# Two transformer blocks on one core: how the relative position bias reaches the attention scores

## The chip, the cores and the metric

The kernel runs on one core of a Trainium2 chip. The metric is the device time of one execution in microseconds (us). The time before is a median of three runs. One further execution was profiled, and every row below is of that execution.

## What is computed

The input x has 256 tokens (T) of 1024 features (D). A first block applies attention and then a mixture of 32 experts (4 chosen per token). A second block applies a gated recurrent mixer, a convolution and a feed-forward part of 2816 features. All is float32. The change touches the attention of the first block alone. Cut to what matters, with 8 heads (H) of 128 features and 256 tokens, it is this:

```python
q, k, v = split(x @ w_in)                       # per head h: 256 x 128 each
s = (q @ k.T) * Dh ** -0.5 + rel_t[h, t5_bucket(qpos - kpos)]
s = where(qpos - kpos >= 0, s, -inf)
p = softmax(s, axis=-1)
t = (p @ v) @ w_out
```

The bias of a head depends on the distance between query and key only, so a head has one row of 512 numbers over all distances. What the products need is that row shifted by one place from query to query: a table of 256 keys for each of 128 queries of a tile.

## The kernel before, in words

The five engines each run a program written out by hand, and wait for each other on semaphores. Time runs through these stages.

**Projections and attention (0 to about 125 us).** The input projection is cut into 12 pieces of 256 columns, r = 0 to 11, in the order q, k, v for each of four pairs of heads (PAIRS). A piece comes by DMA from SP's queue into a ring in SBUF. It is split for exact products: ScalarE rounds it (`split_hi`, L1047), VectorE takes the rest (`split_lo`, L1334). TensorE forms three products per block of 128 (`product`, L562), in two halves of 48 products. Between the halves of the pieces TensorE does the attention of the pairs that are ready: `scores` of a pair in the middle of piece 3 and of the pieces 5, 8 and 11, `turn_probs` (transposes, L544) in the middle of piece 4 and of the later q pieces, `values` (L597, L598) after that. The last pair's transposes stand among the output products (`out_part`, L651).

`scores(h)` (L570) makes both query tiles of a head: queries 0 to 127 see 128 keys, queries 128 to 255 see 256 keys, so a head fills 384 columns of one PSUM bank. Each part has two products into the same bank: a matrix with ones on the anti-diagonal (`const("flip")`) by the bias table (L576, L578), and q by k on top of it (L577, L579). The flip is there because the bias table in SBUF lies with its queries in reverse order. VectorE then takes the row maximum from the bank (`row_max`, L1366, L1367), ScalarE reads the bank, subtracts the maximum, takes the exponential and writes `prob` in SBUF, summing on the way (`exps`, L1077, L1078), VectorE divides by the sum (`normalise`, L1373 to L1375), TensorE transposes.

**The bias table.** TensorE makes the 8 rows of 512 from the buckets (L611), VectorE adds the mask and leaves them in SBUF on 8 partitions (`rel_tab`, L1357). POOL's DMA queue stores them to a scratch tensor in device memory (`rel_rows`, 8 x 512, L501), waits for that (`rel_stored`), and loads the tables back: partition p reads 256 numbers from place p of a head's row on, for heads 0 and 1 (L504, semaphore `bias0_in`) and for heads 2 to 7 (L505, `bias_in`). TensorE waits for `bias0_in` before the scores of head 0 and for `bias_in` before those of head 2. The only other things on POOL's queue in this stage are nine small loads at the start, and after these the rows of the first normalisation (L508, L509), which overwrite the bias tables and so wait for the scores.

**The rest.** The residual and first normalisation, the router, 32 experts whose weights (6 pieces of 2 MB each) stream from SP's queue through a ring of 9 places, then the second block with its own ring. SP loads a new piece into a place when TensorE has used the old one (`piece_done`); four pieces are loaded when the attention's output products are done (`out_ps`).

A `link` is a wait of VectorE for its own last instruction, where the next one reads its result.

Of the kernel before, what the change touches and what calls it, by code (L numbers as in the profile page):

```python
# [10 lines left out]
H = 8  # L11
N_EXP, TOPK, FE = 32, 4, 1024
CAP = 64

EXTRA = T * TOPK // (CAP + 1)
EXTRA_AFTER = 8
# [29 lines left out]

_C = {}
_c = 0
for _name, _width in (("ident", P), ("flip", P), ("before", P), ("ones", P), ("slot", P), ("expert", N_EXP),
                      ("item", EXTRA), ("item64", EXTRA), ("strict", P), ("incl", P), ("own", N_EXP),  # L50
                      ("thresholds", 3), ("index", 1)):
    _C[_name] = (_c, _c + _width)
    _c += _width
# [3 lines left out]
def shape_constants():  # L57

    c = np.zeros((P, CONSTS), np.float32)
    p = np.arange(P)  # L60

    def put(name, value):
        c[:, _C[name][0]:_C[name][1]] = value

    put("ident", np.eye(P))
    put("flip", np.eye(P)[::-1])
    put("before", p[:, None] < p[None, :])
    put("ones", 1.0)
    put("slot", p[None, :] % CAP)
    put("expert", np.arange(N_EXP)[None, :])  # L70
    put("item", np.arange(EXTRA)[None, :])
    put("item64", CAP * np.arange(EXTRA)[None, :])
    put("strict", (p[:, None] < p[None, :] % N_EXP) & (p[:, None] < N_EXP))
    put("incl", (p[:, None] <= p[None, :] % N_EXP) & (p[:, None] < N_EXP))
    put("own", p[:, None] % N_EXP == np.arange(N_EXP)[None, :])
    put("thresholds", CAP * np.arange(1, 4)[None, :])
    put("index", p[:, None])

    levels = np.zeros((P, 1 + len(LEVELS), P), np.float32)
    levels[:, 0] = np.eye(P)  # L80
    for n, m in enumerate(LEVELS):
        same = p[:, None] // (2 * m) == p[None, :] // (2 * m)
        levels[:, n + 1] = same & (p[:, None] % (2 * m) < m) & (p[None, :] % (2 * m) >= m)

    dist = T - 1 - np.arange(2 * T)
    far = np.maximum(dist, 1).astype(np.float32)
    large = 16 + (np.log(far / 16) / np.float32(np.log(8.0)) * 16).astype(np.int32)
    bucket = np.where(dist < 16, dist, np.minimum(large, 31))
    buckets = ((np.arange(32)[:, None] == bucket[None, :]) & (dist >= 0)[None, :]).astype(np.float32)
    behind = np.broadcast_to(np.where(dist < 0, MASKED, 0.0), (H, 2 * T)).astype(np.float32)  # L90
    return c, levels, buckets, np.ascontiguousarray(behind)


def build(nc, x, xT, rel_bias, a_w_in, a_w_out, ln_g, ln_b, w_router, b_router, w_gu, b_gu, w_down, b_down,
# [5 lines left out]
    with ExitStack() as ctx:  # L100
# [159 lines left out]
        extra_in, extra_pe, extra_dve, extra_act = (sem(f"extra_{n}") for n in ("in", "pe", "dve", "act"))  # L260
        w2_in = [sem(f"w2_in{s}") for s in range(W2_PLACES)]
        ln0_in, ln1_in, post_in = sem("ln0_in"), sem("ln1_in"), sem("post_in")
        rel_stored, bias0_in, bias_in = sem("rel_stored"), sem("bias0_in"), sem("bias_in")
        moe_small_in, lev_in = sem("moe_small_in"), sem("lev_in")
        rel_ps, rel_ready = sem("rel_ps"), sem("rel_ready")
        vcol_ps, vcol_ready = sem("vcol_ps"), sem("vcol_ready")
# [219 lines left out]
        def _(pool):  # L486
# [11 lines left out]


            pool.wait_ge(rel_ready, 1)  # L500
            pool.dma_start(rel_rows[:, :], rel_tab).then_inc(rel_stored, 16)  # L501
            pool.wait_ge(rel_stored, 16)
            rel_t = rel_rows.tensor
            pool.dma_start(bias[:, 0:2, :], bass.AP(rel_t, 0, [[1, P], [2 * T, 2], [1, T]])).then_inc(bias0_in, 16)  # L504
            pool.dma_start(bias[:, 2:H, :], bass.AP(rel_t, 4 * T, [[1, P], [2 * T, H - 2], [1, T]])).then_inc(bias_in, 16)  # L505

            pool.wait_ge(s_ps, H)
            pool.dma_start(row_g, row(ln_g[0, :], D)).then_inc(ln0_in, 16)  # L508
            pool.dma_start(row_b, row(ln_b[0, :], D)).then_inc(ln0_in, 16)  # L509
            pool.wait_ge(pt_ps, H)  # L510
# [29 lines left out]
        def _(pe):  # L540
# [27 lines left out]
            pe.wait_ge(xT_lo, 1)  # L568

            def scores(h):  # L570
                if h in (0, 2):
                    pe.wait_ge(bias_in if h else bias0_in, 16)
                if h >= 2:
                    pe.wait_ge(exp_ready, h - 1)
                b = bank[h % 2]
                mm(b[:, 0:P], const("flip"), bias[:, h, P:T], start=True, stop=True)  # L576
                mm(b[:, 0:P], qT[:, h, 0:P], kT[:, h, 0:P], start=False, stop=True, skip_group_check=True)  # L577
                mm(b[:, P:3 * P], const("flip"), bias[:, h, :], start=True, stop=True)  # L578
                mm(b[:, P:3 * P], qT[:, h, P:T], kT[:, h, :], start=False, stop=True,  # L579
                   skip_group_check=True).then_inc(s_ps, 1)  # L580

            def turn_probs(h):
                pe.wait_ge(prob_ready, h + 1)
# [433 lines left out]
        def _(act):  # L1017
# [53 lines left out]

            def exps(h):
                act.wait_ge(max_ready, h + 1)
                if h >= 2:
                    act.wait_ge(pt_ps, h - 1)
                p, s = prob[:, h % 2, :], bank[h % 2]
                activate(p[:, 0:P], s[:, 0:P], ACT.Exp, bias=neg_max[:, h, 0:1], accum_out=prob_sum[:, h, 0:1])  # L1077
                activate(p[:, P:3 * P], s[:, P:3 * P], ACT.Exp, bias=neg_max[:, h, 1:2],  # L1078
                         accum_out=prob_sum[:, h, 1:2]).then_inc(exp_ready, 1)

            def take_probs(h):
# [245 lines left out]
        def _(dve):  # L1327
# [34 lines left out]

            def row_max(h):
                dve.wait_ge(s_ps, h + 1)
                p = bank[h % 2]
                dve.tensor_reduce(neg_max[:, h, 0:1], p[:, 0:P], AX.X, ALU.max, negate=True)  # L1366
                dve.tensor_reduce(neg_max[:, h, 1:2], p[:, P:3 * P], AX.X, ALU.max, negate=True  # L1367
                                  ).then_inc(max_ready, 1)
# [468 lines left out]
```

## Time and profile before

| | |
|---|---|
| median of three runs | 1445.15 us (1445.11 to 1446.24) |
| the profiled execution, its own time | 1446.88 us |
| its span, first to last instruction | 1445.1 us |
| TensorE (PE) busy in products | 1359.8 us, 94% |
| VectorE (DVE) busy | 438.7 us, 30% |
| ScalarE (ACT) busy | 331.5 us, 23% |
| GpSimd (POOL) busy | 57.6 us, 4% |
| mean DMA rate over the span | 334 GB/s |

The page of the profile gives busy times by engine, the span in 40 slices of 36 us, the chain of work that ended last (at each step, what released it), and the costliest groups of instructions. A matmul of float32 operands appears as two records (x2). PEld is the loading of weights into TensorE, which overlaps the products. A row of DMA traffic counts packets; the 4-byte packets that signal semaphores are among those "under 512 B". q1 is SP's queue, q0 is POOL's.

### The profile page before, as it was taken

To read this page: it belongs to the slowest core of one execution; us is meant where nothing else is said; L and a number is where in the kernel's file an instruction comes from. 1 tells how busy PE (TensorE), PEld (TensorE's weight loads), DVE (VectorE), ACT (ScalarE), POOL (GpSimd) and SP (SyncE) were. 2 spreads that over 40 slices of the span, in tenths; PEclk is the share of its full clock that TensorE was granted. 3 is DMA by queue.
4 is the path that set the end of the run, shared out by engine and by line. 5 is a ranking of instruction groups with operands and counts; after the bars stand their busy time and mean duration, and the time that the engine had idled before them with its cause. 6 is when DMAs were issued, how large, how long until landed. Compare 5 with 4: busy or idle time off the path is not lost.

```text
span 1445.1 us, 16969 instructions
## 1 busy us (share of the span) xinstructions
PE 1359.8 (94%) x7356; PEld 727.0 (50%) x7356; DVE 438.7 (30%) x727; ACT 331.5 (23%) x532; POOL 57.6 (4%) x72
## 2 busy tenths in 40 slices
PE   7998999999879999999999999999989878999997
PEld 6996333333223333333333333332349874799975
DVE  4555111001010010010010001100157563677754
ACT  4440101101011011011011000110145421565543
POOL 1001000000000000000000000000000000033310
PEclk9998999999979999999999999999999999999999
DMA  9747899999999999999999999999965400654530
GB/s 376 274 185 289 364 431 430 430 431 430 430 416 430 431 429 431 431 430 431 430 431 430 430 430 431 430 431 431 429 254 204 146 30 0 247 191 176 177 115 30
DMA packets 43738, 483.12 MB, mean 334 GB/s; under 512 B 4652, under 2 KB 4704, under 8 KB 13072
## 3 DMA queue, kind: packets, MB, share of 16 engines
q1 hardware_dynamic: 41824, 476.58, 79.3%
q0 software_dynamic: 1840, 5.44, 1.1%
q8 instruction: 59, 0.97, 0.2%
q14 instruction: 15, 0.12, 0.0%
HBM read 480.94 MB, written 1.06 MB: 334 GB/s over the span
## 4 chain that ended last, share of the span: by engine, by line
PE 79%; DMA 11%; DVE 6%; issue 2%; ACT 2%; SPq 0%; ACTq 0%; DVEq 0%
PE bank L732 25%; PE bank L562 18%; PE bank L740 14%; DMA ring<-in_moe_w_gate_up 10%; PE bank L998 4%; PE bank L752 3%; PE bank L705 3%; PE bank L544 3%; PE bank L724 2%; PE bank L957 2%; PE bank L651 2%; PE bank L918 1%; ACT w_hi L1047 1%; DMA ring<-in_a_w_in 1%; DVE ring L1658 1%
## 5 line engine op out<-in xcount | busy, mean ns | idle before, releaser
L732 PE MATMUL bank<-ring,arena 128*64 128x512 f32 x2048 | 451.9, 597 | 14.1 <-DMA ring<-in_moe_w_gate_up 14.1
L732 PEld LDWEIGHTS bank<-ring,arena 128*64 128x64 f32 x2048 | 143.2, 137 | 321.4 <-issue 291.1
L740 PE MATMUL bank<-ring,arena 128*64 128x512 f32 x1024 | 226.8, 595 | 0.9 <-ACT arena L1149 0.9
L1532 DVE TENSOR_SCALAR arena<-bank 128x512 f32<-128x512 f32 x32 | 22.1, 692 | 669.5 <-PE bank L732 669.5
L562 PE MATMUL bank<-x_hi,w_hi 128*128 128x256 f32 x640 | 185.3, 289 | 13.6 <-DVE w_lo L1348 10.4
L562 PE MATMUL bank<-x_lo,w_hi 128*128 128x256 f32 x640 | 183.0, 286 | 0.0
L562 PE MATMUL bank<-x_hi,w_lo 128*128 128x256 f32 x640 | 182.8, 286 | 0.0
L1334 DVE TENSOR_TENSOR w_lo<-ring,w_hi 128x2048 fp32r<-128x2048 f32 x61 | 139.6, 2291 | 115.0 <-ACT w_hi L1047 115.0
L1047 ACT CAST w_hi<-ring 128x2048 fp32r<-128x2048 f32 x61 | 116.4, 1908 | 117.7 <-PE bank L562 92.9
L740 PEld LDWEIGHTS bank<-ring,arena 128*64 128x64 f32 x1024 | 70.7, 137 | 135.7 <-issue 127.9
L1143 ACT ACTIVATE arena<-arena 128x512 f32<-128x512 f32 x32 | 20.2, 630 | 502.7 <-DVE arena L1532 502.7
L562 PEld LDWEIGHTS bank<-x_hi,w_hi 128*128 128x128 f32 x640 | 124.8, 195 | 15.4 <-issue 11.7
L562 PEld LDWEIGHTS bank<-x_lo,w_hi 128*128 128x128 f32 x640 | 124.9, 195 | 0.0
L562 PEld LDWEIGHTS bank<-x_hi,w_lo 128*128 128x128 f32 x640 | 124.7, 195 | 0.0
L705 PE MATMUL bank<-arena 128*64 128x512 f32 x256 | 62.3, 608 | 11.4 <-issue 10.5
L1156 ACT COPY arena<-bank 128x512 f32<-128x512 f32 x32 | 18.7, 585 | 206.5 <-PE bank L740 206.5
L544 PEld LDWEIGHTS bank<-cst,arena 128*128 128x128 f32 (+1 forms) x396 | 48.1, 186 | 35.1 <-DVE arena L1540 28.0
L752 PE MATMUL bank<-arena 64*128 64x512 f32 x256 | 63.6, 615 | 1.4 <-ACT arena L1156 1.4
L544 PE MATMUL bank<-cst,arena 128*128 128x128 f32 (+1 forms) x396 | 57.4, 291 | 5.6 <-DVE arena L1540 4.2
L1768 DVE SCALAR_TENSOR_TENSOR ring<-ring,vcol 128x256 f32<-128x256 f32 x88 | 48.7, 594 | 0.8
L752 PEld LDWEIGHTS bank<-arena 64*128 64x128 f32 x256 | 22.0, 186 | 42.6 <-issue 39.4
L705 PEld LDWEIGHTS bank<-arena 128*64 128x64 f32 x256 | 18.4, 139 | 47.9 <-issue 46.8
(267 smaller groups left out, 1140.2 us busy)
## 6 DMA issues: line engine op xcount, KB each, us to landing
ring<-in_moe_w_gate_up SPq DMA_DIRECT2D x128, 2048.0 KB, 25.5
ring<-in_moe_w_down SPq DMA_DIRECT2D x64, 2048.0 KB, 27.3
ring<-in_ffn_w_up SPq DMA_DIRECT2D x22, 1024.0 KB, 4.8
ring<-in_w_in SPq DMA_DIRECT2D x14, 1024.0 KB, 6.5
ring<-in_a_w_in SPq DMA_DIRECT2D x11, 1024.0 KB, 19.0
ring<-in_ffn_w_down SPq DMA_DIRECT2D x11, 1024.0 KB, 4.9
ring<-in_a_w_out SPq DMA_DIRECT2D x2, 2048.0 KB, 20.7
ring<-in_w_out SPq DMA_DIRECT2D x2, 2048.0 KB, 8.1
```

The lines of the kernel that those rows point to most:

```text
L544: return pe.transpose(dst, src, ident[0:rows, 0:rows])
L562: last = mm(dst[:, j * T:(j + 1) * T], lhs, rhs, start=c == 0 and n == 0, stop=c == KC - 1 and n == 2)
L651: last = mm(bank[OUT_BANKS[2 * g + t]][:, :], a, w[:, cols], start=h == 0 and k == 0, stop=h == H - 1 and k == 2)
L705: last = mm(bank[2][half * 64:half * 64 + 64, :], sel[:, t, :], h1[:, t, half * 512:(half + 1) * 512], start=t == 0, stop=t == NT - 1)
L724: mm(bank[q][half * 64:half * 64 + 64, :], bias_sel[rows, :], bgu[rows, half, :], start=True, stop=False)
L732: last = mm(bank[q // 2][half * 64:half * 64 + 64, :], chunk(xeT, c), w[:, c % 2, q * 512:(q + 1) * 512], start=False, stop=c == KC - 1)
L740: last = mm(bank[3][half * 64:half * 64 + 64, :], chunk(actT, c), w[:, c % 4, half * 512:(half + 1) * 512], start=c == 0, stop=c == KC - 1)
L752: last = mm(bank[4 + 2 * half + t][:, :], selgT[rows, t, :], y_item[rows, :], start=first, stop=True, skip_group_check=True)
L998: last = mm(bank[2 * t + g][:, :], a, w[:, cols], start=c == 0 and k == 0, stop=c == FB - 1 and k == 2)
L1047: copy(like(w_hi, p), pieces[p][2]).then_inc(hi_ready, 1)
L1334: tt(like(w_lo, p), pieces[p][2], like(w_hi, p).bitcast(f32), ALU.subtract).then_inc(lo_ready, 1)
L1768: last = stt(y[:, g, :], u[:, g, j:j + T], vcol[:, col:col + 1], y[:, g, :], ALU.mult, ALU.add)
```

## The change

The bias is no longer multiplied into the scores. The scratch tensor becomes 8 x 128 x 384: each head's row, cut to its first 384 numbers (REL), is written 128 times, by two stores (heads 0 and 1, then heads 2 to 7). The tables are loaded from it at a stride of 383 numbers per partition, so that partition p begins at place 127 - p of its own copy and the queries lie in their right order. The products with the flip matrix go. VectorE adds the table to the scores as it takes them out of the bank into `prob`, takes the maximum from there, and ScalarE works within `prob`. The waits for the bias move from TensorE to VectorE, so does the wait for the previous use of the `prob` buffer, and the wait that frees a score bank is now for the maximum and not for the exponential. `s_ps` counts scores that TensorE has finished, `max_ready` heads whose maximum is taken.

```diff
+REL = T + P
...
             pool.wait_ge(rel_ready, 1)
-            pool.dma_start(rel_rows[:, :], rel_tab).then_inc(rel_stored, 16)
+            for heads in (slice(0, 2), slice(2, H)):
+                n = heads.stop - heads.start
+                pool.dma_start(rel_rows[heads, :, :], rel_tab[heads, 0:REL].rearrange("h (a n) -> h a n", a=1)
+                               .to_broadcast([n, P, REL])).then_inc(rel_stored if n == 2 else rel_rest, 16)
             pool.wait_ge(rel_stored, 16)
             rel_t = rel_rows.tensor
-            pool.dma_start(bias[:, 0:2, :], bass.AP(rel_t, 0, [[1, P], [2 * T, 2], [1, T]])).then_inc(bias0_in, 16)
-            pool.dma_start(bias[:, 2:H, :], bass.AP(rel_t, 4 * T, [[1, P], [2 * T, H - 2], [1, T]])).then_inc(bias_in, 16)
-
-            pool.wait_ge(s_ps, H)
+            pool.dma_start(bias[:, 0:2, :], bass.AP(rel_t, P - 1, [[REL - 1, P], [P * REL, 2], [1, T]])).then_inc(bias0_in, 16)
+            pool.wait_ge(rel_rest, 16)
+            pool.dma_start(bias[:, 2:H, :], bass.AP(rel_t, 2 * P * REL + P - 1, [[REL - 1, P], [P * REL, H - 2], [1, T]])).then_inc(bias_in, 16)
+
+            pool.wait_ge(max_ready, H)
...
             def scores(h):
-                if h in (0, 2):
-                    pe.wait_ge(bias_in if h else bias0_in, 16)
                 if h >= 2:
-                    pe.wait_ge(exp_ready, h - 1)
+                    pe.wait_ge(max_ready, h - 1)
                 b = bank[h % 2]
-                mm(b[:, 0:P], const("flip"), bias[:, h, P:T], start=True, stop=True)
-                mm(b[:, 0:P], qT[:, h, 0:P], kT[:, h, 0:P], start=False, stop=True, skip_group_check=True)
-                mm(b[:, P:3 * P], const("flip"), bias[:, h, :], start=True, stop=True)
-                mm(b[:, P:3 * P], qT[:, h, P:T], kT[:, h, :], start=False, stop=True,
-                   skip_group_check=True).then_inc(s_ps, 1)
+                mm(b[:, 0:P], qT[:, h, 0:P], kT[:, h, 0:P], start=True, stop=True)
+                mm(b[:, P:3 * P], qT[:, h, P:T], kT[:, h, :], start=True, stop=True).then_inc(s_ps, 1)
...
             def exps(h):
                 act.wait_ge(max_ready, h + 1)
-                if h >= 2:
-                    act.wait_ge(pt_ps, h - 1)
-                p, s = prob[:, h % 2, :], bank[h % 2]
-                activate(p[:, 0:P], s[:, 0:P], ACT.Exp, bias=neg_max[:, h, 0:1], accum_out=prob_sum[:, h, 0:1])
-                activate(p[:, P:3 * P], s[:, P:3 * P], ACT.Exp, bias=neg_max[:, h, 1:2],
+                p = prob[:, h % 2, :]
+                activate(p[:, 0:P], p[:, 0:P], ACT.Exp, bias=neg_max[:, h, 0:1], accum_out=prob_sum[:, h, 0:1])
+                activate(p[:, P:3 * P], p[:, P:3 * P], ACT.Exp, bias=neg_max[:, h, 1:2],
                          accum_out=prob_sum[:, h, 1:2]).then_inc(exp_ready, 1)
...
             def row_max(h):
                 dve.wait_ge(s_ps, h + 1)
-                p = bank[h % 2]
+                if h in (0, 2):
+                    dve.wait_ge(bias_in if h else bias0_in, 16)
+                if h >= 2:
+                    dve.wait_ge(pt_ps, h - 1)
+                s, p = bank[h % 2], prob[:, h % 2, :]
+                tt(p[:, 0:P], s[:, 0:P], bias[:, h, P:T], ALU.add)
+                link(tt(p[:, P:3 * P], s[:, P:3 * P], bias[:, h, :], ALU.add))
                 dve.tensor_reduce(neg_max[:, h, 0:1], p[:, 0:P], AX.X, ALU.max, negate=True)
                 dve.tensor_reduce(neg_max[:, h, 1:2], p[:, P:3 * P], AX.X, ALU.max, negate=True
                                   ).then_inc(max_ready, 1)
...
-    args.append(nc.dram_tensor("rel_rows", (H, 2 * T), mybir.dt.float32, kind="Internal").ap())
+    args.append(nc.dram_tensor("rel_rows", (H, P, REL), mybir.dt.float32, kind="Internal").ap())
```

Besides, the flip matrix leaves the table of constants, which becomes 128 columns narrower.

Three places in the order of instructions follow, first as the program stood before and then as it stands after. On TensorE, in the middle of piece 3, the scores of heads 0 and 1 (`arena` is the SBUF area that holds q, k and the bias, `cst` the constants):

```order
L562 MATMUL bank<-x_hi,w_lo 128x256
L576 MATMUL bank<-arena,cst 128x128 [waits bias0_in,proj_dve,proj_act]
L577 MATMUL bank<-arena 128x128
L578 MATMUL bank<-arena,cst 128x256
L579 MATMUL bank<-arena 128x256
L562 MATMUL bank<-x_hi,w_hi 128x256
```

```order
L566 MATMUL bank<-x_hi,w_lo 128x256
L578 MATMUL bank<-arena 128x128 [waits proj_dve,proj_act]
L579 MATMUL bank<-arena 128x256
L578 MATMUL bank<-arena 128x128
L579 MATMUL bank<-arena 128x256
L566 MATMUL bank<-x_hi,w_hi 128x256
```

The first of these shows the four products of one head (there are as many again for head 1), the second both heads whole: two products of four are left in a head, and the wait for the bias is gone from this engine. On VectorE, after the low parts of the pieces 4 and 5, the softmax of heads 0 and 1:

```order
L1334 TENSOR_TENSOR w_lo<-ring,w_hi 128x2048 [waits hi_ready] x2
L1366 TENSOR_REDUCE arena<-bank 128x1 [waits s_ps]
L1367 TENSOR_REDUCE arena<-bank 128x1
L1373 RECIPROCAL arena<-arena 128x2 [waits exp_ready]
L1374 TENSOR_SCALAR arena<-arena 128x128 [waits dve_step]
L1375 TENSOR_SCALAR arena<-arena 128x256
```

```order
L1331 TENSOR_TENSOR w_lo<-ring,w_hi 128x2048 [waits hi_ready] x2
L1367 TENSOR_TENSOR arena<-bank,arena 128x128 [waits bias0_in,s_ps]
L1368 TENSOR_TENSOR arena<-bank,arena 128x256
L1369 TENSOR_REDUCE arena<-arena 128x1 [waits dve_step]
L1370 TENSOR_REDUCE arena<-arena 128x1
L1367 TENSOR_TENSOR arena<-bank,arena 128x128 [waits s_ps]
L1376 RECIPROCAL arena<-arena 128x2 [waits exp_ready]
L1377 TENSOR_SCALAR arena<-arena 128x128 [waits dve_step]
```

(In the first the two reductions of head 1 are left out, in the second all but the first addition of head 1.) Two additions and a wait for their own result stand ahead of each maximum, and the first addition of head 0 has the wait for the bias. On POOL's queue, between the small loads and the rows of the normalisation:

```order
L497 DMA vrow_b<-in_hgrn_norm_g 4x128
L501 DMA rel_rows<-arena 8x512 [waits rel_ready]
L504 DMA arena<-rel_rows 128x2x256 [waits rel_stored]
L505 DMA arena<-rel_rows 128x6x256
L508 DMA arena<-in_ln_g 128x1024 [waits s_ps]
```

```order
L497 DMA vrow_b<-in_hgrn_norm_g 4x128
L503 DMA rel_rows<-arena 256x1x384 [waits rel_ready]
L503 DMA rel_rows<-arena 768x1x384
L507 DMA arena<-rel_rows 128x2x256 [waits rel_stored]
L509 DMA arena<-rel_rows 128x6x256 [waits rel_rest]
L512 DMA arena<-in_ln_g 128x1024 [waits max_ready]
```

One store of 16 KB has become two of 256 and 768 rows of 1536 bytes, and the second load waits for the second store.

## Rows read from the trace of the kernel before

**Rows 1.** The page: span, busy slices and the chain that ended last.

```profile
span 1445.1 us, 16969 instructions
...
PE   7998999999879999999999999999989878999997
...
DMA  9747899999999999999999999999965400654530
...
PE 79%; DMA 11%; DVE 6%; issue 2%; ACT 2%; SPq 0%; ACTq 0%; DVEq 0%
```

**Rows 2.** The chain in order of time, 30 to 60 us: start, length, what.

```profile
35.33 0.22 PE bank L576 x2
35.55 0.22 PE bank L577 x2
35.77 0.43 PE bank L578 x2
36.20 0.43 PE bank L579 x2
...
37.95 5.75 PE bank L562 x48
43.70 0.66 PE bank L544 x6
```

**Rows 3.** The timeline of DVE and of ACT, 34 to 41 us: start, length, what.

```profile
34.90 2.29 DVE L1334 TENSOR_TENSOR w_lo<-ring,w_hi 128x2048 fp32r<-128x2048 f32 x1 [3.87 <-ACT w_hi L1047]
37.11 0.28 DVE L1366 TENSOR_REDUCE arena<-bank 128x1 f32<-128x128 f32 x1
37.31 0.41 DVE L1367 TENSOR_REDUCE arena<-bank 128x1 f32<-128x256 f32 x1
...
38.70 0.17 DVE L1373 RECIPROCAL arena<-arena 128x2 f32<-128x2 f32 x1
38.90 0.29 DVE L1374 TENSOR_SCALAR arena<-arena 128x128 f32<-128x128 f32 x1
39.10 0.35 DVE L1375 TENSOR_SCALAR arena<-arena 128x256 f32<-128x256 f32 x1
...
37.76 0.37 ACT L1077 ACTIVATE arena<-bank,arena 128x128 f32<-128x128 f32 x1 [2.89 <-DVE arena L1367]
38.47 0.20 ACT L1078 ACTIVATION_READ_ACCUMULATOR arena<-bank,arena 128x1 f32 x1
```

**Rows 4.** The timeline of POOL's queue from 15 us on: start, length of issue.

```profile
18.23 0.50 POOL L501 DMA_DIRECT2D rel_rows<-arena  x1 [12.21 <-DVE arena L1357]
23.13 0.75 POOL L504 DMA_DIRECT2D arena<-rel_rows  x1 [4.41 <-DMA rel_rows<-arena]
23.88 0.87 POOL L505 DMA_DIRECT2D arena<-rel_rows  x1
```

**Rows 5.** DMA issues, 0 to 260 us: count, size, us from issue to landing.

```profile
arena<-rel_rows POOLq DMA_DIRECT2D x1, 768.0 KB, 10.9
arena<-rel_rows POOLq DMA_DIRECT2D x1, 256.0 KB, 7.9
rel_rows<-arena POOLq DMA_DIRECT2D x1, 16.0 KB, 4.6
```

**Rows 6.** DMA traffic in 18:23, the store of the 8 bias rows.

```profile
DMA packets 324, 2.14 MB, mean 428 GB/s; under 512 B 57, under 2 KB 57, under 8 KB 65
...
q0 software_dynamic: 32, 0.02, 1.1%
```

**Rows 7.** DMA traffic in 28:31.5, bias loads beside SP's: packets, MB, share.

```profile
q1 hardware_dynamic: 181, 0.76, 52.8%
q0 software_dynamic: 184, 0.69, 48.0%
```

**Rows 8.** DMA traffic in 34:42, SP's loads of input pieces.

```profile
DMA packets 468, 3.41 MB, mean 426 GB/s; under 512 B 49, under 2 KB 49, under 8 KB 55
...
q1 hardware_dynamic: 466, 3.40, 100.7%
```

**Rows 9.** Stretches 125:135: PE, PEld, DVE, ACT, POOL busy, granted clock.

```profile
125.00:128.20 3.20, 0.30 (x4) 0.09 (x2) 3.06 (x9) 0.88 (x3) 0.00 (x0) 1.00 0.85 251
128.20:131.40 3.20, 3.20 (x17) 3.20 (x18) 3.03 (x5) 0.00 (x0) 0.00 (x0) 0.57 1.02 435
131.40:135.00 3.60, 3.60 (x6) 1.43 (x7) 0.00 (x0) 0.00 (x0) 1.07 (x2) 0.50 1.01 432
```

**Rows 10.** DMA traffic in 124:170, 40 slices of 1.15 us, GB/s.

```profile
GB/s 0 199 256 442 456 427 427 385 413 417 477 388 470 370 452 353 477 406 470 385 488 46 14 0 0 214 228 442 427 442 427 399 427 456 399 442 456 427 442 427
```

More of the change, by code:

```diff
@@ L48 @@
 _c = 0
-for _name, _width in (("ident", P), ("flip", P), ("before", P), ("ones", P), ("slot", P), ("expert", N_EXP),
+for _name, _width in (("ident", P), ("before", P), ("ones", P), ("slot", P), ("expert", N_EXP),
                       ("item", EXTRA), ("item64", EXTRA), ("strict", P), ("incl", P), ("own", N_EXP),
@@ L65, in shape_constants @@
     put("ident", np.eye(P))
-    put("flip", np.eye(P)[::-1])
     put("before", p[:, None] < p[None, :])
@@ L262, in build @@
         ln0_in, ln1_in, post_in = sem("ln0_in"), sem("ln1_in"), sem("post_in")
-        rel_stored, bias0_in, bias_in = sem("rel_stored"), sem("bias0_in"), sem("bias_in")
+        rel_stored, rel_rest, bias0_in, bias_in = sem("rel_stored"), sem("rel_rest"), sem("bias0_in"), sem("bias_in")
         moe_small_in, lev_in = sem("moe_small_in"), sem("lev_in")
```

## The prediction

> **What bounds the kernel now.** I read the page first. TensorE is busy 9 tenths or more nearly throughout and holds 79% of the chain; DMA holds 11%, and its slices are full through the experts [rows 1]. So two resources run close together, and the question is which of them sets the end of the stage that the change touches. The chain in order of time answers that for the attention: from 35 to 60 us it is TensorE alone, product after product, with no wait in it, and the flip products stand in it with the rest [rows 2]. In this stretch whatever is taken from TensorE is taken from the path, and whatever makes it wait is added.
>
> The next question is whether a shift survives the experts, which DMA paces. The traffic of 124 to 170 us shows it [rows 10]: the stream is at zero when the attention ends, fills the free places of the ring, falls to 46, 14, 0 and 0 GB/s at 148 to 153 us, and starts for good when TensorE has used the first expert's first piece. The long stream thus hangs on the end of the attention. A change of that end moves the rest of the program as a whole, and I carry it to the end at full size.
>
> About 0.2% of the time, 2.9 us, is what a measurement of this kernel can tell from no change.
>
> **What is removed.** The flip products of a head take 0.22 + 0.43 us on the chain [rows 2]. Eight heads: 8 x 0.65 = **-5.2 us**, 1.3 us in each pair. All of it is on the path.
>
> **What VectorE gets.** Two additions per head, 128 and 256 columns wide. The trace has no such addition; the nearest rows are the scalings of the same widths, 0.20 us from start to start and 0.35 us for the second [rows 3], so 0.55 us a head. Doubling that is my upper bound, nothing the lower, since a pass over the same data can't be free but may overlap. The two reductions take 0.2 + 0.41 us. A head's `row_max` is then 1.2 us, a pair's 2.4. Behind the second head's come ScalarE's two exponentials, 37.76 to 38.67, 0.95 us with the hand-over, and VectorE's reciprocal and scalings, 38.70 to 39.45, 0.8 us [rows 3]. From the moment when VectorE can start on a pair to the moment when both heads are ready for the transposes: 2.4 + 0.95 + 0.8 = 4.1 us. What hides it is the half piece of 5.75 us on TensorE in between. VectorE started at 37.11, after the low part of piece 5, and TensorE's transposes at 43.70 [rows 2, 3], which is now 42.4 since the flip products of the pair are gone. That leaves 5.3 us for 4.1: hidden, with 1.2 us to spare, in the first pair as in the later ones, whose rows repeat this pattern. Cost 0; at the upper bound, 1.1 us more, still about 0. The same spare time is what is left if the cover shrinks.
>
> **What the DMA queue gets.** This is where I put the weight. Before, POOL stored 16 KB at 18.23 and it landed 4.6 us later; the loads were issued at 23.13 and 23.88 and landed after 7.9 and 10.9 us, at 31.0 and 34.8 [rows 4, 5]. The scores of head 0 began at 35.33 [rows 2], so the bias was there 4.3 us early. Now the bias of heads 0 and 1 is needed by VectorE. Working back from the transposes: head 1 must be ready at 42.4 + 0.33 = 42.7, so the bias must have landed by 42.7 - 4.1 = **38.6 us**. Every microsecond beyond that is a microsecond of TensorE.
>
> The first store is 2 x 128 rows of 1536 bytes, 0.39 MB, out of 2 partitions; the second 6 x 128 rows, 1.18 MB, out of 6. How fast they go depends on how many of the 16 DMA engines share them. The store before had 8 rows on 8 partitions, and it shows as exactly 8 packets between 2 and 8 KB: the packets under 8 KB are 65, those under 2 KB 57, out of 32 on q0 [rows 6]. One packet per partition row, nothing cut further. I read this as a spread that follows the rows of the source. Then the new stores go out over 2 and 6 engines, and each engine has 128 rows, 196 KB.
>
> On such an engine the store does not run alone: SP's loads alone fill all 16 engines at 34 to 42 us [rows 8]. While both queues had work, q0 had 184 packets and q1 181 in 3.5 us [rows 7]: they take turns packet by packet. The same row gives 1.45 MB in 3.5 us, 26 GB/s for one engine, 0.16 us for 4 KB. A packet of SP's input pieces is 8 KB (3.40 MB in 466 less 49 packets) and takes 0.31 us at 426 / 16 = 26.6 GB/s [rows 8]. The bias loads' rows of 1 KB went four to a packet of 4 KB, so I let two store rows share one of 3 KB, 0.115 us. An engine then takes 64 turns. Sixteen of them meet the 4 KB packets of x (1 MB over 16 engines), 48 the 8 KB ones: 48 x 0.425 + 16 x 0.275 = 24.8 us. The bounds: 7.4 us if SP's loads don't slow it (196 KB at 26.6 GB/s), and 34.9 us if each row is a packet of its own (64 turns as above with 0.058 us for the row are 21.1, and 64 more against 4 KB packets of the output weights are 13.8).
>
> The first store lands at 18.23 + 4.6 + 24.8 = 47.6, the load is issued 0.3 later as before, and lands after 7.9 at **55.8 us**. The second store has as many rows per engine and ends with it; its load lands at about 59.5, long before head 2 is reached. VectorE holds the queue meanwhile: behind it stand the low part of piece 6 and ScalarE's exponentials with the eviction of q, but TensorE needs none of these before piece 6, and stops first at the transposes in the middle of piece 4. Its stall is 55.8 + 4.1 - 42.7 = **+17.2 us**.
>
> The Trainium skill, *DMA: Bandwidth & Descriptors*, section on why a DMA increments its semaphore by 16, speaks against this change in the same way: a DMA is spread over the largest number up to 16 that divides the slowest dimension of both its sides. By it the stores would use 2 and 6 engines; that the trace's 8 packets agree is all that can be seen here.
>
> A stall has a second price. After the 3.2 us in which TensorE was all but idle at 125, its granted clock was 0.57 and then 0.50, the lower level of 1.2 GHz, for 6.8 us [rows 9]. Half of 6.8 us is lost, **+3.4 us**. After a longer stall I expect the same once; the bounds are 0 (if the clock is back by then) and the same twice.
>
> **Sum.** -5.2 + 0 + 17.2 + 3.4 = +15.4 us. Against the profiled execution, 1446.9, that is 1462.3 us; that execution lay 1.7 us above the median of the runs, so against the median it is 1460.5. With so rough a term I say **1460 us**. The later wait for the loads of the normalisation's rows (now behind `max_ready`, some 4 us after the scores rather than 0) is hidden behind the output products, and four engines' other work is unchanged: 0.
>
> **The rivals.**
>
> *The stores spread wide (faster).* If 16 engines share them, an engine has 8 packets of the first store, 3.4 us with turns, landing at 26.2. The load is queued behind the second store's 24 packets, 10.2 us, then 4 packets of its own at 0.47 us: 38.3 us, just before 38.6. No stall, -5.2 us: 1440 us. For it: SP's loads keep all engines full [rows 8], and the destination has 256 rows. Against it: the 8 packets. It decides at a landing of 38.6 us. The same page's fit for a DMA of this queue, 2 us plus the bytes at 436 GB/s, would land the first store in 2.9 us and also give this result; the trace's 16 KB took 4.6 [rows 5], and beside loads the fit leaves out the turns. Chance 0.29.
>
> *Narrow, row by row.* Each row is its own packet: 10 us later still, +25.5 us, 1470.5 us. For it: nothing shows rows of 1536 bytes being joined. Chance 0.12.
>
> *Narrow, but hardly slowed by SP's loads.* The store lands between 30 and 38, the bias between 38 and 46, the stall is 0 to 7 us: about 1444 us. Against it: the turns of [rows 7]. Chance 0.06.
>
> *The shift is swallowed.* The experts' stream absorbs the change either way, 1445 us, if its restart hung on something else than TensorE. Against it: the gap in [rows 10]. Chance 0.05.
>
> **How the numbers follow.** The forecast has 0.48. The range runs from the wide case to a little beyond the row-by-row case, 1439 to 1472. Since cases of both signs hold the chance, the forecast's own range is 1452 to 1468. Faster: the wide case and half of the fourth, 0.31. Within 0.2%: the swallowed case and part of the fourth, 0.07. Slower: 0.62.
>
> **What would show it.** Right: the store `rel_rows<-arena` of 384 KB takes near 29 us to land, POOL's first load is issued near 48 us, VectorE's first addition starts near 56 us after an idle time laid to that load, TensorE is idle from about 42 to 59 us before the transposes, and a stretch of half clock follows. No flip products, 16 of the additions, and the later pairs without a wait. Wrong: VectorE's first addition at 37 us, right behind the low part of piece 5, and an unbroken chain on TensorE. The size is wrong if the landing lies elsewhere than at 48; then the stall moves with it, one for one.

## The result, and the profile after

The changed kernel takes **1473.24 us** (median of 4 runs, 1471.64 to 1473.79) against 1445.13 us before in the same comparison: a ratio of 1.0191, 95% interval 1.0178 to 1.0203. It is slower by 28 us. I had forecast 1460 us, slower by 15, with a range up to 1472. The sign and the place were right, the size was not. Where no number of runs is given below, a time is of one execution.

The profiled execution took 1473.79 us, 26.9 more than that of before, as do the spans. The page after, against [rows 1]:

```profile
span 1472.0 us, 16922 instructions
...
PE   7199899999969999999999999999989978999997
...
PE 76%; DMA 14%; DVE 6%; issue 2%; ACT 2%; SPq 0%; ACTq 0%; DVEq 0%
```

The second slice of TensorE, 36 to 72 us, has gone from 9 to 1, and DMA's share of the chain from 11% to 14%. The chain in order of time, against [rows 2], says which DMA (start, length, what):

```profile
16.58 0.69 DVE arena L1354
17.27 0.28 issue
17.55 27.48 DMA rel_rows<-arena
45.04 0.28 issue
45.32 23.02 DMA arena<-rel_rows
...
68.44 0.29 DVE arena L1367
...
72.74 0.90 PE bank L548 x3
73.65 7.12 PE bank L566 x48
```

From 17.55 to 68.3 us the program's end hangs on two transfers, the first store and the load of heads 0 and 1. The issues by size give all four, in KB and us to landing, against [rows 5]:

```profile
rel_rows<-arena POOLq DMA_DIRECT2D x1, 1152.0 KB, 48.3
...
arena<-rel_rows POOLq DMA_DIRECT2D x1, 768.0 KB, 8.3
...
rel_rows<-arena POOLq DMA_DIRECT2D x1, 384.0 KB, 27.5
arena<-rel_rows POOLq DMA_DIRECT2D x1, 256.0 KB, 23.0
```

VectorE waited 31.93 us for the load before its first addition, and TensorE 29.89 us for VectorE before the transposes of head 0, then 0.24 before those of head 1:

```profile
68.44 0.29 DVE L1367 TENSOR_TENSOR arena<-bank,arena 128x128 f32<-128x128 f32 x1 [31.93 <-DMA arena<-rel_rows]
...
71.60 0.90 PE L548 MATMUL bank<-cst,arena 128*128 128x128 f32 x3 [29.89 <-DVE arena L1378]
72.74 0.90 PE L548 MATMUL bank<-cst,arena 128*128 128x128 f32 x3 [0.24 <-DVE arena L1378]
```

The later pairs have no such wait. And the shift is carried to the end whole: the first long run of expert products stood at 148.37 us in the chain of before and stands here at 175.13, 26.8 us later, of 26.9 in the span. The line of before, then that of the changed kernel:

```profile
148.37 13.91 PE bank L732 x64
```

```profile
175.13 13.91 PE bank L731 x64
```

So the first store landed at 45.0 us, where I had 47.6. The load is what I had wrong: 23.0 us from issue to landing, not 7.9. The second store landed at 66.9 us, 22 us after the first, where I had the two end together.

### The profile page after: what moved, and what is told of

Read it like the earlier page. It is cut to its first block, busy times and chain, and to the rows that moved or that the text cites. A ratio compares the mean times of both kernels' runs of the same rounds, so it can differ in the third digit from the quotient of the medians.

```text
span 1472.0 us, 16922 instructions
## 1 busy us (share of the span) xinstructions
PE 1357.0 (92%) x7324; PEld 724.2 (49%) x7324; DVE 442.9 (30%) x743; ACT 332.1 (23%) x532; POOL 58.9 (4%) x73
## 3 DMA queue, kind: packets, MB, share of 16 engines
q0 software_dynamic: 3216, 7.01, 1.7%
## 4 chain that ended last, share of the span: by engine, by line
PE 76%; DMA 14%; DVE 6%; issue 2%; ACT 2%; SPq 0%; ACTq 0%; DVEq 0%
PE bank L731 25%; PE bank L566 16%; PE bank L739 13%; DMA ring<-in_moe_w_gate_up 10%; PE bank L997 4%; PE bank L751 3%; PE bank L704 3%; PE bank L548 3%; PE bank L723 2%; DMA rel_rows<-arena 2%; DMA arena<-rel_rows 2%; PE bank L956 2%; PE bank L650 1%; PE bank L917 1%; ACT w_hi L1046 1%
## 5 line engine op out<-in xcount | busy, mean ns | idle before, releaser
L548 PE MATMUL bank<-cst,arena 128*128 128x128 f32 (+1 forms) x396 | 58.2, 292 | 35.7 <-DVE arena L1378 30.1
L704 PE MATMUL bank<-arena 128*64 128x512 f32 x256 | 62.2, 608 | 11.5 <-issue 10.5
L704 PEld LDWEIGHTS bank<-arena 128*64 128x64 f32 x256 | 18.4, 139 | 48.0 <-issue 46.9
## 6 DMA issues: line engine op xcount, KB each, us to landing
ring<-in_moe_w_down SPq DMA_DIRECT2D x64, 2048.0 KB, 26.6
```

Of the source, the lines that this page charges most:

```text
L548: return pe.transpose(dst, src, ident[0:rows, 0:rows])
L704: last = mm(bank[2][half * 64:half * 64 + 64, :], sel[:, t, :], h1[:, t, half * 512:(half + 1) * 512], start=t == 0, stop=t == NT - 1)
```

## The experiments

Two questions were open. Is the arithmetic as cheap as forecast, with the whole loss in the DMAs? And why did the load take 23 us and the second store 48?

**1. The small store again** (`small_store`): the changed kernel's arithmetic with the store and loads of before. It leaves out that the tables' queries are put in the right order.

```diff
-            for heads in (slice(0, 2), slice(2, H)):
...
+            pool.dma_start(rel_rows[:, :], rel_tab).then_inc(rel_stored, 16)
+            pool.wait_ge(rel_stored, 16)
+            pool.dma_start(bias[:, 0:2, :], bass.AP(rel_t, 0, [[1, P], [2 * T, 2], [1, T]])).then_inc(bias0_in, 16)
+            pool.dma_start(bias[:, 2:H, :], bass.AP(rel_t, 4 * T, [[1, P], [2 * T, H - 2], [1, T]])).then_inc(bias_in, 16)
```

> The changed kernel with the store and loads of before (16 KB, 8 rows; the tables then lie with their queries in reverse, so this kernel leaves out the un-reversing of the bias). If the whole loss comes from the 1.57 MB of stores and what waits for them, the bias lands near 31 us, VectorE starts on head 0 at about 36.5 us behind the low part of piece 5, TensorE has no wait before its transposes, and the time is that of before less 5.2 us of flip products and less the 0.7 us by which the changed kernel's start is earlier: about 1439 us. If instead the additions on VectorE or the softmax within prob cost time in every pair, a wait shows before each pair's transposes and the time is 1441 us or more.

Measured: 1439.22 us (8 runs), ratio 0.9965 (0.9953 to 0.9976) to 1445.05 before. The chain at the first pair:

```profile
34.34 0.22 PE bank L574 x2
34.57 0.43 PE bank L575 x2
35.00 0.22 PE bank L574 x2
35.22 0.43 PE bank L575 x2
35.66 5.75 PE bank L562 x48
41.41 0.66 PE bank L544 x6
```

Two products of four are left per head, and the transposes follow the 48 products with no wait, here as in the other pairs. The arithmetic gains what was forecast; all of the loss lies in the DMAs.

**2. The load on another queue** (`act_load`). The load of heads 0 and 1 goes to ScalarE's queue, and the bias rows get a place of their own in SBUF, since `prob` would overwrite them there.

```diff
-            pool.dma_start(bias[:, 0:2, :], bass.AP(rel_t, P - 1, [[REL - 1, P], [P * REL, 2], [1, T]])).then_inc(bias0_in, 16)
...
+                    act.wait_ge(rel_stored, 16)
+                    act.dma_start(bias[:, 0:2, :], bass.AP(rel_rows.tensor, P - 1, [[REL - 1, P], [P * REL, 2], [1, T]])).then_inc(bias0_in, 16)
```

> The changed kernel with the load of heads 0 and 1 issued from ScalarE's own DMA queue when the first store has landed (45 us), the second store as it was, and rel_tab in a place of its own. Queue theory (the load takes 23 us since it stands behind the second store on POOL's queue of every engine): it now lands in 8 to 10 us, at 53 to 55 us, VectorE's first addition moves from 68.4 to about 54 us, and the time falls by 13 to 15 us to about 1459 us. Rival (the load is slow because memory or the engines are clogged by the second store's packets, whatever the queue): it lands near 68 us again and the time stays at 1473 us.

Measured: 1473.93 us, and the load took 22.6 us: the queue theory in this form fell.

```profile
arena<-rel_rows ACTq DMA_DIRECT2D x1, 256.0 KB, 22.6
```

The traffic of the new queue (q10), in 50:55 and in 60:65, shows what happened instead:

```profile
q10 hardware_dynamic: 137, 0.13, 7.4%
...
q10 hardware_dynamic: 21, 0.02, 1.2%
```

The load is cut into packets of 1 KB. More than half of it moved within 5 us, then it crept at 21 packets in 5 us, while the second store was still running. An engine busy with the second store lets a foreign packet in once per turn, and its turns were long. Standing behind the store's packets or among them made no difference to the time. That their slowness was the matter is argued here; the next runs test it.

**3. The rows on distant partitions** (`spread_src`): each head's row is made on 16 partitions, by a wider stationary operand, and the stores read partitions 0, 16, 32 and so on. Everything else of the stores is the same.

```diff
+            dve.tensor_copy(relb16, relb_sb.rearrange("p (h a) -> p h a", a=1).to_broadcast([32, H, 16])
+                            ).then_inc(rel_ready, 1)
...
-                pool.dma_start(rel_rows[heads, :, :], rel_tab[heads, 0:REL].rearrange("h (a n) -> h a n", a=1)
+                pool.dma_start(rel_rows[heads, :, :], rel_tab[16 * heads.start:16 * heads.stop:16, 0:REL]
+                               .rearrange("h (a n) -> h a n", a=1)
```

> The bias rows stand on partitions 0, 16, 32 to 112 in place of 0 to 7; both stores still have 2 and 6 source rows of 128 copies. Port theory (the second store's packets take up to 1 us because six engines read out of the same few neighbouring partitions): its packets fall to about 0.17 us, the second store lands near 53 us in place of 66.9, the load of heads 0 and 1 near 55, the time is near 1459 us. Rival (the packets are slow on the side of device memory, or from their number): both land where they did, 66.9 and 68.3 us, 1473 us. Both theories leave the first store's landing at about 45 us, since its turns with SP's packets stay.

Measured: 1457.92 us. TensorE's stall is 15.1 us in place of 29.9.

```profile
rel_rows<-arena POOLq DMA_DIRECT2D x1, 1152.0 KB, 33.5
...
rel_rows<-arena POOLq DMA_DIRECT2D x1, 384.0 KB, 21.9
arena<-rel_rows POOLq DMA_DIRECT2D x1, 256.0 KB, 13.9
```

The second store and the load are as the port theory had them. The first store was not: it, too, became faster, 21.9 us against 27.5. Its rows on partitions 0 and 1 had shared the path with the second store's on 2 and 3. POOL's queue traffic in 38:42, in the changed kernel and then here:

```profile
q0 software_dynamic: 175, 0.19, 35.4%
```

```profile
q0 software_dynamic: 186, 0.27, 18.1%
```

More bytes in half the engine time. Yet the second store still landed at 52.6 us, 12.7 us after the first at 39.9: distance took away only a part of the gap between them.

**4. At a distance of four** (`spread4`): the same with copies on 4 partitions and the stores reading 0, 4, 8 to 28.

```diff
-                pool.dma_start(rel_rows[heads, :, :], rel_tab[16 * heads.start:16 * heads.stop:16, 0:REL]
+                pool.dma_start(rel_rows[heads, :, :], rel_tab[4 * heads.start:4 * heads.stop:4, 0:REL]
```

> As the kernel with rows on partitions 0, 16, 32 and so on, but the bias rows stand on partitions 0, 4, 8 to 28. If neighbours within a group of four partitions share one path for DMA, every row now has a path of its own and the second store's packets are as fast as at a distance of 16: the second store lands near 52 us after 33 to 34 us, the time is 1457 to 1459 us. If what matters is the distance over the whole 128 partitions (a path shared by 16 or 32 neighbours), the packets are slow again, and the time is nearer to 1473 us.

Measured: 1456.77 us, and the load took 12.6 us.

```profile
rel_rows<-arena POOLq DMA_DIRECT2D x1, 1152.0 KB, 32.4
```

Four partitions of distance do all that sixteen do.

**5. All engines** (`wide`): 16 copies of each row as in 3, but every one of these partitions is a source, writing 8 copies. The bytes and their place in memory are the changed kernel's.

```diff
-                pool.dma_start(rel_rows[heads, :, :], rel_tab[heads, 0:REL].rearrange("h (a n) -> h a n", a=1)
-                               .to_broadcast([n, P, REL])).then_inc(rel_stored if n == 2 else rel_rest, 16)
+                pool.dma_start(rel_rows[heads, :, :].rearrange("h (a b) n -> (h a) b n", a=16),
+                               rel_tab[16 * heads.start:16 * heads.stop, 0:REL]
+                               .rearrange("h (a n) -> h a n", a=1).to_broadcast([16 * n, 8, REL])).then_inc(rel_stored if n == 2 else rel_rest, 16)
```

> Each head's row stands on 16 partitions, and each partition writes 8 copies: 32 and 96 source partitions, the same bytes in the same layout. If the spread over engines follows the rows of the source, all 16 engines now carry 16 rows of the first store and 48 of the second: the first lands near 26 us, the second near 34, the load of heads 0 and 1 near 36, just in time, and the time is 1439 to 1441 us. If the loss were in the amount written (1.57 MB beside SP's loads) and not in its spread, the first store would still land after 35 us and the time stay above 1450 us.

Measured: 1441.30 us (10 runs), ratio 0.9976 (0.9965 to 0.9987): faster than before.

```profile
rel_rows<-arena POOLq DMA_DIRECT2D x1, 1152.0 KB, 15.1
...
rel_rows<-arena POOLq DMA_DIRECT2D x1, 384.0 KB, 7.3
arena<-rel_rows POOLq DMA_DIRECT2D x1, 256.0 KB, 10.3
```

VectorE's first addition stands at 36.21 us, right behind the low part of piece 5, and no transposes wait. In 22:26 POOL's queue moved this much in the changed kernel, and here:

```profile
q0 software_dynamic: 219, 0.09, 7.9%
```

```profile
q0 software_dynamic: 151, 0.57, 34.9%
```

Six times the bytes beside the same loads of SP. So neither the amount written nor SP's traffic alone is the trouble, but the number of source partitions and their place.

**6. The load ahead of the second store** (`swap`).

```diff
+                if heads.start:
+                    pool.wait_ge(rel_stored, 16)
+                    pool.dma_start(bias[:, 0:2, :], bass.AP(rel_t, P - 1, [[REL - 1, P], [P * REL, 2], [1, T]])).then_inc(bias0_in, 16)
```

> POOL's queue issues the load of heads 0 and 1 before the second store, and the second store after it; rel_tab has a place of its own. If the load took 23 us only because of the second store's packets (ahead of it in POOL's queue, or taking turns with it in another), it now lands 8 to 10 us after its issue at 45 us, at 53 to 55, and VectorE's first addition is at about 54 us. The second store then begins near 50 us and lands late, past 70 us, so that a second wait appears before the scores of heads 2 and 3 are taken; the total is between 1460 and 1475 us. If the load still takes over 15 us, something other than the second store slows it (memory, or SP's loads alone).

Measured: 1476.64 us, just above the expected range. The first store landed after 22.0 us, the load after **6.7**, the first addition came at 46.6 us, earlier than expected. The second store, begun at 40.6, took 40.9, and TensorE waited twice:

```profile
arena<-rel_rows POOLq DMA_DIRECT2D x1, 256.0 KB, 6.7
...
49.77 0.90 PE L549 MATMUL bank<-cst,arena 128*128 128x128 f32 x3 [8.06 <-DVE arena L1379]
...
90.19 0.90 PE L549 MATMUL bank<-cst,arena 128*128 128x128 f32 x3 [22.54 <-DVE arena L1379]
```

That settles the load: without the second store it takes no longer than it took before, and the 16 us on top are the second store's.

**7. SP's queue held** (`sp_held`): the load of x and all after it wait for both stores.

```diff
+            sp.wait_ge(rel_rest, 16)
             sp.wait_ge(xT_lo, 2)
```

> SP's queue waits for both stores to land before it loads x and the pieces from 8 on; the eight pieces already issued still run until about 28 us. If the first store's 27.5 us are mostly turns with SP's 8 KB packets (0.31 us against 0.18 for its own), it lands near 33 to 35 us in place of 45. The second store's packets stay slow if their slowness comes from the shared source partitions (landing after 45 us), and fall to 0.18 us if it came from sharing with SP's loads (landing before 42 us). The load of heads 0 and 1 follows the second store. Time 1450 to 1465 us in the first case, 1440 to 1447 in the second.

Measured: 1463.14 us. The first store did not land earlier but at 46.9 us, after 29.4; my expectation for it was wrong. The second took 39.9 in place of 48.3. The traffic of 34:38, with SP silent, is the clearest reading of the study:

```profile
DMA packets 43, 0.20 MB, mean 50 GB/s; under 512 B 0, under 2 KB 0, under 8 KB 43
...
q0 software_dynamic: 43, 0.20, 46.9%
```

46.9% of 16 engines over 4 us is 30 us of engine time for 43 packets of 4.6 KB: 0.70 us each, with nothing else moving. Eight engines together moved 50 GB/s, about what two carry elsewhere (26.6 each in [rows 8]). The 8 source rows stood on partitions 0 to 7, two groups of four. Whether each group has a path of its own, or all eight have one of 50 GB/s, shows at the end of the second store in the changed kernel, long after the first has landed. In 62:66 POOL's queue moved 0.10 MB in 4 us, half as much, 25 GB/s, which is what one group gets if the four rows of partitions 4 to 7 are the last to be done (the trace doesn't name the partitions):

```profile
q0 software_dynamic: 21, 0.10, 18.4%
```

The first store's late landing fits this too. With SP's packets gone, the second store starts sooner on its engines and slows the first for longer. In 28:32 POOL's queue moved 0.09 MB in the changed kernel (the lines stand below, under the spread over engines) and 0.29 MB here:

```profile
q0 software_dynamic: 425, 0.29, 53.9%
```

**8. Both** (`swap_held`): as 6, with SP's queue held until the first store has landed, so that this store is alone in its last part.

```diff
+            sp.wait_ge(rel_stored, 16)
             sp.wait_ge(xT_lo, 2)
```

> The kernel with the second store behind the first load, and SP's queue held until the first store has landed (the eight input pieces already issued run until about 28 us). The first store is now alone with its own turns: if it took 22.0 us there because its 43 packets per engine took turns with SP's, it needs about 12 turns of 0.49 us until 28 us and then 31 packets of 0.18 us alone, and lands near 34 us, 16 to 17 us after its issue; the first additions on VectorE stand at about 41 us and its first stall is 2 to 3 us in place of 8.1. If turns with SP's packets don't matter to it, it takes 22 us again and the stall stays 8 us. The late bias of heads 2 to 7 remains in either case; the time is 1468 to 1480 us.

Measured: 1477.02 us; the first store took 19.2 us against 22.0 in 6, the first stall was 7.3 us. I had expected a landing near 34 us, and it came at 37.2. The trace gives two reasons. I had counted the pieces already issued as done at 28 us on every engine, but on the store's two engines they are themselves delayed by the turns: SP's queue still moved 8 packets in 30:32, and none in 32:34. And then the store did not run at full speed to its end. POOL's queue in 32:34 and in 34:36, with no other packet in either:

```profile
q0 software_dynamic: 22, 0.10, 14.2%
...
q0 software_dynamic: 10, 0.05, 11.0%
```

The first is 0.21 us for a packet and 51 GB/s for the two engines, the second 0.35 us and 23 GB/s. So two rows on neighbouring partitions also came down to about what one engine moves, but not at once. Why the first 2 us or so ran at twice that rate stays open.

**9. No large store at all** (`revcols`): the small store and the loads of before; the row of 8 x 512 is built for distances in rising order, and VectorE reads the table's keys backwards.

```diff
-    dist = T - 1 - np.arange(2 * T)
+    dist = np.arange(2 * T) - P + 1
...
-                tt(p[:, 0:P], s[:, 0:P], bias[:, h, P:T], ALU.add)
-                link(tt(p[:, P:3 * P], s[:, P:3 * P], bias[:, h, :], ALU.add))
+                tt(p[:, 0:P], s[:, 0:P], bias[:, h, 0:P][:, ::-1], ALU.add)
+                link(tt(p[:, P:3 * P], s[:, P:3 * P], bias[:, h, ::-1], ALU.add))
```

> A full version without the large stores: the table of 8 rows is built in the reverse order of distances (two constants tables change), stored once (16 KB) and loaded as before, and VectorE reads the bias with its keys backwards (a step of -1 along the free dimension) when it adds. If a backward read costs VectorE nothing, its additions take 0.29 and 0.41 us as in the changed kernel, the bias lands near 30 us, and the time is that of the kernel with the small store, 1439 us, 5.5 to 6 us below before. If a backward read is slower, the additions grow, and with over 0.25 us more per addition a wait shows before each pair's transposes.

Measured: **1438.56 us** (5 runs), ratio 0.9950 (0.9936 to 0.9963) to 1444.85 before. It is the full computation, and the fastest of the kernels here that are. The backward reads:

```profile
35.91 0.28 DVE L1363 TENSOR_TENSOR arena<-bank,arena 128x128 f32<-128x128 f32 x1
36.11 0.41 DVE L1364 TENSOR_TENSOR arena<-bank,arena 128x256 f32<-128x256 f32 x1
```

as long as the forward ones of the changed kernel, 0.29 and 0.41 us, and in their place right behind the low part of piece 5.

## Why the prediction was right in sign and wrong in size

**The flip products, -5.2 us: right.** `small_store` gives 5.8 us less than before, with an interval of some 3.5 to 6.8 that holds it. The changed kernel's issue of the store was 0.7 us earlier than before, 17.55 against 18.23 us [rows 4]. In the runs that leave the making of the bias rows as it is, this issue stood anywhere from 17.0 to 18.0 us, so I make nothing of it beyond the sum below.

**The additions, 0: right.** They took 0.29 and 0.41 us. From VectorE's start on a pair to both heads ready: 68.44 to 72.7, 4.3 us, forecast 4.1. With the bias in time, no wait appeared in any pair (`small_store`, `wide`, `revcols`).

**The spread over engines: right.** The step from "8 packets for 8 rows" to 2 and 6 engines for the new stores carried the sign. `wide` shows it from the other side, with 32 and 96 source rows. The rule that I named, from the Trainium skill, *DMA: Bandwidth & Descriptors*, on the increment by 16, held. The traces add a detail: the whole program's packets on POOL's queue, 1840 before, are 3216 in the changed kernel and 2240 in `wide`:

```profile
q0 software_dynamic: 3216, 7.01, 1.7%
```

```profile
q0 software_dynamic: 2240, 7.25, 1.4%
```

The 976 packets more are almost all tiny (in 22:27 of the changed kernel 275 of 538 packets are under 512 B). An engine that has no row of a narrow store gets a tiny packet for each that the others carry, and on each of them a turn is taken with SP's. The traffic of the changed kernel in 28:32 shows the turns, as many packets on one queue as on the other:

```profile
q1 hardware_dynamic: 308, 1.50, 95.6%
q0 software_dynamic: 308, 0.09, 9.6%
```

The forecast had no such packets, and they have a price: the second store's engines first work off the first store's tiny ones, 43 turns with SP's packets of 0.31 us [rows 8], an estimate of 13 us. No run takes these packets away alone, so this price is argued.

**The first store, 29.4 us forecast, 27.5 measured: near by luck, since two errors cancelled.** Its packets hold three rows, not two (0.20 MB in 43 packets, 4.6 KB, `sp_held`), so it has 43 turns on an engine and not 64. Alone with SP's loads it took 22.0 us (`swap`). The other 5.5 us came from the second store on neighbouring partitions (21.9 without them, `spread_src`).

**The load, 7.9 us forecast, 23.0 measured: the step that failed.** I wrote that the second store "has as many rows per engine and ends with it". Both halves of the reasoning behind that were wrong. On POOL's queue the load stands behind the second store on the six engines that carry it. I used this order in the rival with wide stores, and left it out of the forecast, since I took both stores to end together. And the second store did not end with the first, but 22 us later. Two things held it up. It began late, behind the first store's tiny packets: in 28:32 the queue moved 0.09 MB, the share of the two engines of the first store, and where the rows stand apart it still ended 12.7 us (`spread_src`) or 11.5 us (`spread4`) after the first. And its six engines read out of partitions 2 to 7, which gives the other 9 us: four neighbours together got about 25 GB/s (`sp_held`, and 62:66 above), what one engine moves alone. Nothing in the trace of before could show the second: its store had the same 8 partitions, but one packet each. The load's excess over the forecast is 15.1 us. With the second store away the load takes 6.7 us, so all of it is that store's (`swap`); with the rows 16 partitions apart it takes 13.9, so 9.1 of it go with the shared path (`spread_src`), and the rest goes with the order on the queue and the late start.

The Trainium skill has this path, which I did not look up: *SBUF — State Buffer*, the section on the DMA port swizzle, says that the four partitions of a group share one of 16 ports, and that each port serves two such groups, 32 partitions apart. `spread4` agrees with the first (a distance of four was enough), and so do the 50 GB/s for two groups. The second is not seen here: by it the rows of `spread_src` stood two to a port, and its second store took 33.5 us against 32.4 in `spread4`. The 51 GB/s out of partitions 0 and 1, a single group, in 32:34 of `swap_held` stay unexplained.

**The stall, +17.2 us forecast, 29.9 + 0.24 = 30.1 measured.** The first store landed 2.6 us earlier than forecast, and the load took 15.1 us more. TensorE stood at its transposes at 41.7 us and not at 42.4, which adds 0.7 to its wait.

**The clock, +3.4 us forecast.** After the stall the granted clock was at its lower level of 1.2 GHz, then back (PE, PEld, DVE, ACT, POOL busy, clock), against [rows 9]:

```profile
41.00:72.70 31.70, 1.61 (x9) 1.00 (x8) 3.71 (x14) 2.76 (x10) 1.63 (x2) 0.58 0.67 216
72.70:76.00 3.30, 3.26 (x15) 3.26 (x16) 1.79 (x1) 1.48 (x1) 0.00 (x0) 0.50 0.25 104
76.00:80.00 4.00, 4.00 (x32) 4.00 (x32) 1.19 (x2) 2.07 (x3) 0.00 (x0) 0.92 0.05 19
```

The 48 products behind it took 7.12 us and not 5.75, 1.4 us more, and the transposes 0.90 us for each head where both together had 0.66 [rows 2], 1.1 us more: 2.5 us in all. The mean of 0.58 in 41:72.7 shows that most of the slow stretch lay within the stall, where it cost nothing. The sum: -5.2 + 30.1 + 2.5 = +27.4, less the 0.7 us by which TensorE came to its transposes early, is +26.7. The spans differ by 26.9.

**The rivals.** The fast one, "spread wide", was false for this kernel and true to 1.3 us for the kernel that spreads (`wide`, 1441.3 against 1440). The row-by-row one came near the time, 1470.5, by a mechanism that isn't there: the packets are larger, not smaller. My range ended at 1472, at the edge of that rival, and had no room for a slower second store, a transfer that I had priced only by its own bytes.

## What to carry to other kernels

A broadcast store out of few partitions ran here on as many DMA engines as it had source rows, the other engines got tiny packets that held up the next store, and neighbours among four shared one path: make the copies on chip first, or give every engine a source partition. A transfer on a queue is priced by all that stands ahead of it there, also when it is small. And a change of order that costs a large transfer can often be had by an access pattern: reading backwards on VectorE cost nothing here.

## What the runs showed of the hardware that I had not expected

- DMA out of SBUF: eight engines reading partitions 0 to 7 moved 50 GB/s together, 0.70 us for a packet of 4.6 KB with nothing else running; with the rows at a distance of 4 or 16 partitions the second store took 32.4 or 33.5 us and not 48.3.
- Where a store uses only some engines, the others get tiny packets in the same number, and take turns on them (308 packets of POOL's queue beside 308 of SP's in 28:32, with 0.09 MB against 1.50).
- Two engines reading partitions 0 and 1 with nothing else running moved 51 GB/s in 32:34 and 23 GB/s in 34:36 (`swap_held`).
- The same load was cut into packets of 4 KB on POOL's queue and of 1 KB on ScalarE's (137 packets for 0.13 MB, against 184 for 0.69 MB in [rows 7]), so it needs four times as many turns there.
- VectorE's addition of a PSUM and an SBUF operand took 0.28 and 0.41 us for 128 and 256 columns with a step of +1 and of -1 alike.
